# Latent attention: another order of the projections, and more matmuls inside the head loop

## What is computed

```python
def mla(hn, positions, w_in, q_norm_g, w_uq, kv_norm_g, w_ukv, w_out):
    proj = hn @ w_in                                    # 1024 -> 384 + 256 + 64
    cq, ckv, k_rope = jnp.split(proj, [MLA_Q_RANK, MLA_Q_RANK + MLA_KV_RANK], axis=-1)
    q = (rmsnorm(cq, q_norm_g) @ w_uq).reshape(B_, S_, H, MLA_QK)            # 128 + 64 a head
    kv = (rmsnorm(ckv, kv_norm_g) @ w_ukv).reshape(B_, S_, H, MLA_NOPE + MLA_V)
    q_nope, q_rope = jnp.split(q, [MLA_NOPE], axis=-1)
    k_nope, v = jnp.split(kv, [MLA_NOPE], axis=-1)
    ...
    q_rope = rotate(q_rope, cos, sin)
    k_rope = rotate(k_rope[:, :, None, :], cos, sin)    # one for all heads
    q = jnp.concatenate([q_nope, q_rope], axis=-1)
    k = jnp.concatenate([k_nope, jnp.broadcast_to(k_rope, (B_, S_, H, MLA_ROPE))], axis=-1)
    ...
        s = jnp.einsum('bqhd,bkhd->bhqk', q_blk, k).astype(jnp.float32) * scale
        s = jnp.where(kpos[None, :] <= qpos[:, None], s, -jnp.inf)
        p = jax.nn.softmax(s, axis=-1).astype(v.dtype)
        return jnp.einsum('bhqk,bkhd->bqhd', p, v)
    ...
    return o.reshape(B_, S_, H * MLA_V) @ w_out         # 1024 -> 1024
```

## Time and profile before

| what | us |
|---|---|
| median of 3 runs | 1675.87 (1675.41 to 1678.34) |
| the profiled execution, its time | 1674.19 |
| its span, first to last instruction | 1672.4 |
| PE busy in the span | 1563.0 (93%) |
| DVE busy | 1185.0 (71%) |
| ACT busy | 775.1 (46%) |
| POOL busy | 481.1 (29%) |
| mean granted clock of PE | 0.962 |

### The profile page before, as it was taken

The page is one execution under the profiler, slowest core; times in us unless marked ns, Lnnn a source line. Parts: engine busy times, 40 slices in busy tenths (PEclk is TensorE's granted clock), DMA queues, the critical chain, the costliest instruction groups (busy, mean ns, idle before and its releaser), DMA issues. The chain is left out here.

```text
span 1672.4 us, 24237 instructions
## 1 busy us (share of the span) xinstructions
PE 1563.0 (93%) x10372; PEld 1417.4 (85%) x10372; DVE 1185.0 (71%) x1231; ACT 775.1 (46%) x863; POOL 481.1 (29%) x262
## 2 busy tenths in 40 slices
PE   6999999999999999999999798359999998999998
PEld 6899999888889999998888697238888896788886
DVE  6656766788655567668898876965888566479863
ACT  5333554666443344546664252105665442456642
POOL 2704200245210051004758700441344000024520
PEclk9999999999999999999999898779999997899999
DMA  7574345455545542454555333004455542145552
GB/s 262 179 276 154 126 152 177 177 180 198 179 174 178 189 154 110 163 190 177 182 190 201 120 128 125 0 0 151 176 184 188 183 158 101 51 154 199 177 182 95
DMA packets 43687, 265.07 MB, mean 158 GB/s; under 512 B 4379, under 2 KB 9755, under 8 KB 14652
## 3 DMA queue, kind: packets, MB, share of 16 engines
q1 hardware_dynamic: 43580, 263.52, 44.5%
HBM read 259.31 MB, written 4.19 MB: 158 GB/s over the span
## 5 line engine op out<-in xcount | busy, mean ns | idle before, releaser
L1105 DVE TENSOR_TENSOR w_lo<-raw,w_hi 128x2048 fp32r<-128x2048 f32 (+2 forms) x246 | 590.9, 2404 | 204.3 <-ACT w_hi L816 202.4
L816 ACT ACTIVATE w_hi<-raw 128x2048 fp32r<-128x2048 f32 (+2 forms) x246 | 460.0, 1871 | 329.1 <-PE gemm L480 230.4
L480 PE MATMUL gemm<-x_two,w_hi 128*128 128x256 f32 x2176 | 403.4, 288 | 8.5 <-DVE x_two L1114 4.4
L480 PEld LDWEIGHTS gemm<-x_two,w_hi 128*128 128x128 f32 x2176 | 346.2, 196 | 11.5 <-issue 6.1
L480 PE MATMUL gemm<-x_two,w_lo 128*128 128x256 f32 x1088 | 311.5, 286 | 0.0
L480 PEld LDWEIGHTS gemm<-x_two,w_lo 128*128 128x128 f32 x1088 | 212.7, 196 | 0.0
L1669 POOL TENSOR_TENSOR tmp<-tmp 128x512 f32<-128x512 f32 x24 | 36.7, 1529 | 530.9 <-ACT tmp L842 530.6
L507 PE MATMUL gemm<-y_two,w_hi 128*128 128x512 f32 x484 | 170.6, 398 | 5.8 <-DVE w_lo L1105 5.8
L507 PE MATMUL gemm<-xb_two,w_hi 128*128 128x512 f32 x480 | 169.3, 401 | 2.1 <-DVE w_lo L1105 2.1
L507 PE MATMUL gemm<-x_two,w_hi 128*128 128x512 f32 x464 | 162.3, 399 | 2.1 <-DVE w_lo L1105 2.1
L1754 POOL TENSOR_TENSOR cv<-cv,rstd 128x512 f32<-128x512 f32 x44 | 107.8, 2450 | 172.9 <-ACT cv L895 172.5
(11 more groups left out here) (344 smaller groups left out, 2977.2 us busy)
## 6 DMA issues: line engine op xcount, KB each, us to landing
raw<-in_weights SPq DMA_DIRECT2D x226, 1024.0 KB, 4.8
raw<-in_weights SPq DMA_DIRECT2D x16, 768.0 KB, 4.3
bias_table<-tab SPq DMA_DIRECT2D x3, 1024.0 KB, 5.3
bm<-bias_table SPq DMA_DIRECT2D x8, 384.0 KB, 6.2
raw<-in_weights SPq DMA_DIRECT2D x4, 576.0 KB, 3.7
h<-in_x SPq DMA_DIRECT2D x1, 1024.0 KB, 5.7
out_y<-tmp SPq DMA_DIRECT2D x4, 256.0 KB, 2.2
ang<-in_s_abt SPq DMA_DIRECT2D x3, 264.0 KB, 15.3
```

The source lines that it names most:

```text
L480: mm = pe.matmul(out, lhs, rhs, start=fresh and m == 0, stop=end and m == 2, skip_group_check=True)
L816: me.give(act.activation(w_hi[i % SPL][:, 0:n], raw[i % RAW][:, 0:n], ACT.Copy), w_hi_ready)
L1105: me.give(v.tensor_tensor(w_lo[i % RAW][:, 0:n], raw[i % RAW][:, 0:n], w_hi[i % SPL][:, 0:n].bitcast(F32), ALU.subtract), w_lo_ready)
```

## The change

The columns of mp are put in another order, so that its first block holds the latents of keys and values, its second the rotary key and the first chunk of the queries, its third the other two chunks. ukv is divided into uk (keys, 2 blocks of 1024) and uv (values, 2 blocks of 1024). The list becomes uk0, uv0, uq0, uk1, uq1, uq2, uv1, uq3.

The two norms are summed, rooted and inverted apart: keys and values after mp1, queries after uk0 (`latent_sums`, `inverse`). The rotation is done for the key and for each pair of heads apart (`turned`, `turned_q` on PE, `rope`, `rope_q` on DVE). Only uk0, uv0, uq0, uk1 and uq1 run before the head loop. uq2, uv1 and uq3 run inside it, in iterations 0, 1 and 2 (`BETWEEN`), and with each of them, one iteration later, comes the eviction and the split of a block three ahead: mo0, mo1 and mo2. The blocks mo0 and mo1 are also computed in the loop, chunk by chunk, as each head's output is there (`mo_chunk`, from iteration 3, 12 matmuls each); the last chunk follows the loop. After it come mo2, mo3 and the FFN as before. The arithmetic is the same.

```diff
-    plan += [Block("uq", 0, 384, 3, ftiles(384, 3), 2) for _ in range(4)]
-    plan += [Block("ukv", 0, 1024, 2, ...
+    uq = [Block("uq", 0, 384, 3, ftiles(384, 3, 3), 2) for _ in range(4)]
+    uk = [Block("uk", 0, 512, 2, ftiles(512, 2), 2) for _ in range(2)]
+    uv = [Block("uv", 0, 512, 2, ttiles(512, 2), 2) for _ in range(2)]
+    plan += [uk[0], uv[0], uq[0], uk[1], uq[1], uq[2], uv[1], uq[3]]
...
+BETWEEN = {0: ("uq", 2), 1: ("uv", 1), 2: ("uq", 3)}
...
             for j in range(3):
                 gemm(first("mp") + j, x_hi, x_lo, BY_PAIR if j == 0 else ())
                 if j == 0:
                     norm(tokens=False)
-            for j in range(4):
-                gemm(first("uq") + j, xb_hi, xb_lo, {0: (x_ready, 1), 2: (x_ready, 1)} if j == 0 else ())
...
+                if j == 1:
+                    latent_sums((0, 1), S, 2 * S)
+            gemm(at("uk", 0), xb_hi, xb_lo, {0: (x_ready, 1)})
+            latent_sums((2, 3, 4), 2 * BANK)
+            pe.wait_ge(read_out, PLAN[first("mp") + 1].out)
+            turned(c6[:, 2, :])
+            gemm(at("uv", 0), xb_hi, xb_lo)
+            gemm(at("uq", 0), xb_hi, xb_lo, {3: (x_ready, 1), 4: (x_ready, 1)})
+            gemm(at("uk", 1), xb_hi, xb_lo)
             me.take(rope_ready)
-            pe.wait_ge(read_out, PLAN[first("ukv") + 1].out)
+            turned_q(0)
+            gemm(at("uq", 1), xb_hi, xb_lo)
+            me.take(rope_ready)
...
+            def mo_chunk(c):
+
+                head_read(c)
+                for i in (first("mo"), first("mo") + 1):
...
+                    if c == 0:
+                        pe.wait_ge(w_lo_ready, i + 1)
+                        pe.wait_ge(read_out, b.freed)
...
             m_scores(0)
             for j in range(MH + 2):
+                if j == 0:
+                    turned_q(1)
+                if j == 1:
+                    me.take(rope_ready)
+                if j == 2:
+                    turned_q(2)
                 if j + 1 < MH:
                     m_scores(j + 1)
+                if j == 4:
+                    head_read(1)
+                    turned_q(3)
+                if j in BETWEEN:
+                    gemm(at(*BETWEEN[j]), xb_hi, xb_lo)
+                if j >= 3:
+                    mo_chunk(j - 3)
                 if j >= 2:
                     hd = j - 2
                     me.take(pt_ready)
                     if hd:
-                        me.take(pv_read)
+                        head_read(hd - 1)
+                    if hd in (0, 2):
+                        me.take(rope_ready)
...
-            me.take(pv_read)
-            for j in range(4):
+            mo_chunk(MH - 1)
+            for j in range(2, 4):
                 gemm(first("mo") + j, x_hi, x_lo)
...
                     me.give(act.activation(pm[:, :], A[:, 2 * BANK:2 * BANK + 3 * P], ACT.Copy), pt_ready)
+                if j - 1 in BETWEEN:
+                    split_next(at(*BETWEEN[j - 1]))
             feed_after(first("mo"), named("ffn.1"), xb_hi)
...
+            latents(0, (0, 1), "kv_g", 0)
+            latents(1, (3,), "q_g", 3)
+            inverse(S, 2 * S + 2)
+            latents(2, (4, 5), "q_g", 3)
+            keys(0)
+            rope(kr[:, 0, :], c6[:, 2, :], tmp[:, 4, :])
+            inverse(0, S)
+            values(0)
+            queries(0)
+            keys(1)
+            rope_q(0)
+            queries(1)
...
                 if 1 <= j <= MH:
                     m_soft_b(j - 1)
+                if j in (0, 2, 4):
+                    rope_q(1 + j // 2)
+                if j - 1 in BETWEEN:
+                    kind, k = BETWEEN[j - 1]
+                    filled[kind](k)
                 if j >= 2:
                     me.take(pv_hi)
```

More of the change, by code:

```diff
@@ L731, in _, with latent_sums, turned, turned_q @@
             ffn(2)
+            def latent_sums(cs, o, tokens=None):
+                me.take(sq_ready)
+                m = None
+                for c in cs:
+                    m = pe.matmul(A[:, o:o + S], ones[:, :], sqm[:, c, :], start=c == cs[0], stop=c == cs[-1],
+                                  skip_group_check=True)
+                for t in range(ST if tokens is not None else 0):
+                    for c in cs:
+                        m = pe.matmul(A[:, tokens + t:tokens + t + 1], sqm[:, c, t * P:(t + 1) * P], ones[:, 0:1],
+                                      start=c == cs[0], stop=c == cs[-1], skip_group_check=True)
+                me.give(m, ms_ready)
+            TURNED = 3 * BANK + S
+            def turned(src):
+                me.give(pe.matmul(A[:, TURNED:TURNED + S], rotate, src, start=True, stop=True, skip_group_check=True),
+                        rot_ready)
+            def turned_q(j):
+                pe.wait_ge(read_out, PLAN[at("uq", j)].out)
+                turned(rx[:, j, :])
             for j in range(3):
@@ L775, in m_scores, with head_read @@
                 me.give(m, scores_ready)
+            heads_before = me.taken.get(pv_read.name, 0)
+            def head_read(hd):
+                pe.wait_ge(pv_read, heads_before + hd + 1)
+            def mo_chunk(c):
+                head_read(c)
+                for i in (first("mo"), first("mo") + 1):
+                    b = PLAN[i]
+                    wh = w_hi[i % SPL][:, 0:b.used].rearrange("p (c n) -> p c n", c=DC)
+                    wl = w_lo[i % RAW][:, 0:b.used].rearrange("p (c n) -> p c n", c=DC)
+                    if c == 0:
+                        pe.wait_ge(w_lo_ready, i + 1)
+                        pe.wait_ge(read_out, b.freed)
+                    for t in range(2):
+                        o, n = b.bank * BANK + t * S, slice(t * P, (t + 1) * P)
+                        two = ((wh[:, c, n], x_hi[:, c, :]), (wh[:, c, n], x_lo[:, c, :]), (wl[:, c, n], x_hi[:, c, :]))
+                        for m, (lhs, rhs) in enumerate(two):
+                            mm = pe.matmul(G[:, o:o + S], lhs, rhs, start=c == 0 and t == 0 and m == 0,
+                                           stop=c == DC - 1 and m == 2, skip_group_check=True)
+                    if c == DC - 1:
+                        me.give(mm, mm_done)
             m_scores(0)
             for j in range(MH + 2):
+                if j == 0:
[4 more added lines that the diff above has]
+                    turned_q(2)
                 if j + 1 < MH:
                     m_scores(j + 1)
+                if j == 4:
[5 more added lines that the diff above has]
+                    mo_chunk(j - 3)
                 if j >= 2:
@@ L1592, in _, with inverse @@
-            me.settle()
-            me.give(v.tensor_copy(small[:, 45:46], small[:, 0:1]), rx_ready)
-            cb = cos_r[:, :, :].to_broadcast([P, 4, S])
-            sb_ = sin_r[:, :, :].to_broadcast([P, 4, S])
-            v.tensor_tensor(tmp[:, 0:4, :], rx[:, :, :], cb, ALU.mult)
-            me.give(v.tensor_tensor(tmp[:, 4, :], c6[:, 5, :], cos_r[:, 0, :], ALU.mult))
-            i = first("ukv")
-            for j in range(2):
-                p = psum(i + j)
+            def inverse(a0, a1):
+                me.take(rms_ready)
+                me.give(v.reciprocal(rstd[:, a0:a1], rstd[:, a0:a1]))
+                me.settle()
```

114 lines of the change are left out of this document (51 added, 63 removed).

## The result

The changed kernel takes 1679.78 us (median; 1678.96 to 1682.52) where the kernel before takes 1676.1 in the same comparison (1675.41 to 1678.48). The ratio is 1.0021, 95% interval 1.0014 to 1.0029: slower by 3.7 us, small but measurable. One execution of the changed kernel, 3077.76 us, was disturbed and is left out. The forecast of 1675.7 us missed by 4.1 us; the time lies in the range given, on the side of rival C, but not by rival C's mechanism.

The account below looks back on a forecast made before the run. PE was taken to bound the latent attention, with 13.6 us idle and a loop largely at 1.2 GHz. Terms -2.9, +2.2 and +0.5 sum to -0.2 us, about 1674.0; plus 1.68 to the median, 1675.7 us, range 1671 to 1684.

Parts of the forecast that it names:

- rival C: Head loop: clock falls at the 6.1 us gap and stays down until the chunks end; about 1684 us, chance 0.23.
- the path to the first scores: Projections before the head loop: 33.0 us instead of 52.5, so head 0's scores start near 1386.4, 19.5 us earlier.
- the circle in the loop: Iterations 1 to 3: splits on ACT and DVE delay PE, idling 2.2, 6.1 and 3.4 us; gives back 16.6 of 19.5.
- the output blocks: Behind the loop: ACT and DVE rounds start up_a0 19.4 us after mo0's end; taking mo1 out (5.76 us) gains nothing.
- 0.9 + 7.4 us: Behind the loop: PE's predicted idle before up_a0, with only mo2 and mo3 left to compute.
- the clock of the changed kernel: Head loop and up_a0: lower granted clock adds 2.2 us in the loop and 0.5 us at up_a0.
- the walk: Step-by-step pricing of the stage at 2.4 GHz: mo0 ends at 1450.3 instead of 1453.2, -2.9 us.
- the 6.1 us gap: Head loop: PE's idle before the first mo chunk, expected to drop the clock for about 10 us, costing 2.2 us.
- the 13.6 us at 1.00: Old head loop: full clock held despite waits of 0.6 to 1.0 us, taken as partly contradicting the Trainium skill's rule.
- the base of the sum: Whole kernel: profiled 1674.19 us changed by -0.2 to about 1674.0, plus 1.68 to the median, gives 1675.7 us.
- within 0.2%: Whole kernel: a difference under 3.35 us, about indistinguishable by measurement; chance 0.52.
- the second circle: Behind the loop: ACT and DVE alternate over four rounds of h, 6.19 us each, setting when up_a0 starts.

Follow-up runs that it names:

- experiment 3: Changed kernel with ACT's high part of the weight block moved ahead of x_hi and the probabilities copy in iterations 1 to 3: 1669.88 us, ratio 0.9955.
- experiment 5: Kernel before with only the output-block chunks put into its head loop: 1680.35 us; the same with reordered ACT and DVE work behind the loop: 1670.16 us.
- experiment 4: Changed kernel with ACT and DVE reordered behind the loop (two h at once, earlier high parts): 1672.19 us; also with the early high part in the loop: 1662.9 us.
- c_after2: Changed kernel, unedited, profiled again; reached the latent attention early, at 1352.76 us: 1674.56 us.
- c_before: Kernel before, unedited, profiled a second time; reached the latent attention late, at 1360.10 us: 1677.64 us.
- f1_chunks_only: Kernel before with only the first two output blocks computed in chunks inside the head loop: 1680.35 us, ratio 1.0013.
- the three kernels with the new order: ACT and DVE reordered behind the loop: on the changed kernel 1672.19 us, with the early high part too 1662.9, on the kernel before with chunks 1670.16.

## Why the prediction was wrong

**Right: the path to the first scores.** Forecast 1386.4; in the trace 1395.71, which is 1386.81 with the 8.90 us of the late arrival taken off. The waits of 0.7 and 1.4 us ahead of it were 0.4 and 1.7, and the 0.3 before the scores did not show.

**Right: the circle in the loop.** Its three waits came out at 2.33, 6.19 and 3.15 us; experiment 3 shows that ACT's split behind the copy is what makes them.

**Right: the output blocks.** It is 19.36 us from the first h to up_a0, with a wait of 7.0 us at its end; experiment 5 isolates it, experiment 4 takes it away. The forecast's idle of "0.9 + 7.4 us" is 0.4 us more than its own sum leaves (19.4 less 11.5 for mo2 and mo3).

**Right in size, and half right in form: the clock of the changed kernel.** At 2.4 GHz throughout the forecast was 2.9 us below before, so a stage of 116.95. Inside the stage the clock was priced at 2.2. What was measured above the 116.95, the walk's own errors included, is 2.8 us after the early arrival (119.78) and 1.9 after the late ones (118.83). The other 0.5 us, for up_a0, falls into the rest, which takes 199.9 to 200.3 us against 199.7 to 200.1 before. The fall that was put at the 6.1 us gap is there after a late arrival; after the early one (c_after2) it came already at the 2.33 us wait. Rival C, which kept the clock down until the chunks end, did not occur: 0.92 over the loop.

**Misread: the 13.6 us at 1.00.** The prediction read in the earlier trace rows that "1.00 held over 13.6 us with waits of 0.6 to 1.0 us in them". But PE has no wait in the first 8.3 us of that stretch. The three waits (0.64, 1.04 and 0.64 us) lie in its last 5.3 us, and the clock falls where it ends:

```profile
1436.70:1442.00 5.30, 2.98 (x18) 2.24 (x17) 3.55 (x14) 3.03 (x11) 0.00 (x0) 1.00 0.00 0
1442.00:1448.40 6.40, 4.84 (x21) 4.00 (x19) 0.85 (x2) 1.26 (x3) 0.00 (x0) 0.51 0.01 3
```

Five of the six traces of before show this fall, and c_before does not. The changed kernel's last four chunks follow waits of 0.60, 0.61, 0.60 and 1.02 us, and the clock held: 1.00 over the 19.8 us from 1440.0 to 1459.8. So small waits alike in size were followed by a fall in most traces of one loop and by none in this trace of the other. The prediction had set its reading against a rule of the Trainium skill (TensorE: Matmul & The Clock Gate, section "A second HAM failure mode: psum-queue depth-cycling"), by which frequent small idles between groups that change banks make the clock swing. The rows of before agree with that rule rather than contradict it; the changed kernel's do not show it.

**Wrong: the base of the sum.** The prediction said: "The profiled execution took 1674.19, so about 1674.0; the median of the runs is 1.68 us above it, so the forecast is 1675.7 us." That shift carries the time from one execution to the median as if both kernels moved alike. They do not. The profiled execution was one of the early arrivals. In it upstream is 5.7 to 8.9 us faster than in the late ones of both kernels, and before's stage about 4 us slower; its total hides much of that, because the two go against each other. Against this execution the forecast of -0.2 us was good: at the same arrival the spans are 1672.4 and 1672.8, the stage 119.85 and 119.78. Against a late one the same change costs 3.4 us, because before's stage then takes 115.3 to 116.0 and the changed one's 118.8.

The sign of this was in the earlier trace rows. They showed 0.58 behind a gap of 2.14 us, and 20.4 us at 0.50. I used both as fixed costs of the kernel before and priced the clock's uncertainty for the changed kernel alone, where it was 0 to +11 us. What the change took out of the projections, two falls of some 1.5 us each, is only one after a late arrival. No rival said that before's own stage can be 4 us shorter than in its trace, as it was in three of six, so the chances were set too tightly on "within 0.2%". "What follows up_a0 should be unchanged to 1 us" held (199.8 and 200.0 on the median trace), and "a gain or a loss of the stage goes into the span whole" held too.

**What stays open.** Why the clock falls behind one gap in one execution and not behind the same gap in the next was not found, nor why the arrival goes with it. The share of executions of before with the long stage was not measured, so that the medians differ by 3 to 4 us for this reason is an inference from the traces.

## What to carry to other kernels

Where a stage's time depends on the granted clock, one profiled execution is one draw. Take its falls behind short gaps as costs that may or may not be there, and give them a range in the *old* kernel too. A profiled total near the median does not say that its parts are near theirs. Moving matmuls into another engine's circle gains nothing until the circle itself is cut: here the same added work cost 3 us with ACT's split behind the copy it delays, and brought 8 us with the split a few instructions earlier, and 13 with the second circle cut as well. Look for which engine's *order* closes the circle; putting one instruction ahead of two others, in three iterations, was worth more than moving 20 us of matmuls.

## What was not expected of the hardware

The clock's falls are not a property of the program alone: the same program, with the same 2.14 us gap, ran the 4.10 us behind it at 0.58 in one execution and at 1.00 in another, and the same instruction was reached between 1352.6 and 1360.1 us in the kernel before and between 1352.8 and 1361.6 in the changed one. And a wait at a block's start can cost twice. Behind waits of 2.12 us (before) and 7.0 us (after) PE ran the first 20 us of up_a0 fully busy at 0.91, and at 0.85 behind the 7.0 us of f1_chunks_only; behind the 0.83 to 1.69 us of the three kernels with the new order it ran them at 1.00. In the rest of the span that is 1.2 to 2.8 us. The loss did not follow the length of the wait alone: 2.12 and 7.0 us were followed by the same 0.91.
